# A hybrid decoder layer on one core: another order around block B's groups, output rows turned back in pieces, decay and outer product in one operation

## The reference, cut to what matters

```python
def hybrid_layer(x, ...):
    h = rmsnorm(x, norm_mix_g)
    ...                                    # one projection of h feeds two mixers
    S_new, o_g = gla(...)                  # gated linear attention, per token: S = diag(a) S + k^T v,  o = q S
    o_d = diff_attn(...)                   # samples read a paged cache of 2048 keys and values each
    x = x + concat(o_g, o_d) @ w_out
    h2 = rmsnorm(x, norm_ffn_g)
    u = square(relu(h2 @ w_up))            # 1024 -> 4096
    return x + u @ w_down                  # 4096 -> 1024
```

## Time and profile before

| what | value |
|---|---|
| median of 3 runs | 1423.88 us (1423.36 to 1424.85) |
| the profiled execution | 1431.62 us, its span 1429.9 us |
| PE busy | 1364.5 us (95%), 8589 matmuls |
| DVE, ACT, POOL busy | 923.8, 579.3, 402.4 us |
| mean granted TensorE clock | 0.988 of full speed |
| chain that ended last | PE 54%, DVE 8%, ACT 4%, DMA 3% |
| DMA | mean 168 GB/s |

### The profile page before, as it was taken

One profiled execution on the slowest core, in us unless ns is written; L12 is line 12 of the kernel. 1 busy time (PEld: TensorE's weight loads), 2 busy tenths in 40 slices (PEclk: granted clock), 3 DMA queues, 4 the chain that ended last, 5 costly groups with the idle time before them and its releaser, 6 DMA issues.

```text
span 1429.9 us, 23899 instructions
## 1 busy us (share of the span) xinstructions
PE 1364.5 (95%) x8589; PEld 1130.2 (79%) x8589; DVE 923.8 (65%) x1625; ACT 579.3 (41%) x1081; POOL 402.4 (28%) x395
## 2 busy tenths in 40 slices
PE   7999999999999999998999999999998999999998
PEld 6767777776777767776766767667998999999998
DVE  5459757745657877648667565434456665777885
ACT  6444333314545553624234241323433554334532
POOL 2546614335533444352000000000332112320330
PEclk9999999999999999999999999999999999999999
DMA  7537735344345574567386575873553563233021
GB/s 267 152 119 233 227 115 165 122 149 133 98 140 169 198 261 127 185 224 235 120 269 229 178 255 182 274 242 120 182 196 118 207 211 114 89 119 115 34 90 60
DMA packets 125527, 240.33 MB, mean 168 GB/s; under 512 B 13593, under 2 KB 46650, under 8 KB 125410
## 3 DMA queue, kind: packets, MB, share of 16 engines
q1 hardware_dynamic: 116210, 214.69, 45.4%
q10 hardware_dynamic: 9200, 24.13, 5.1%
HBM read 197.64 MB, written 41.14 MB: 167 GB/s over the span
## 4 chain that ended last, share of the span: by engine, by line
PE 54%; DVE 8%; issue 4%; ACT 4%; DMA 3%; SPq 1%; POOL 1%; ACTq 0%; DVEq 0%; POOLq 0%
PE ps L85 16%; PE ps L87 15%; PE ps L86 15%; PE ps L3258 2%; PE ps L1495 2%; DMA vr<-in_cache_v 1%; PE ps L1532 1%; DVE uw_l L2020 1%; PE ps L1314 1%; DMA kr<-in_cache_k 1%; ACT uw_h L2014 1%; DVE part_l L2784 1%; DVE xt L2793 1%; PE ps L1516 1%; DMA raw_dn<-in_w_down 1%
## 5 line engine op out<-in xcount | busy, mean ns | idle before, releaser
L3023 POOL TENSOR_TENSOR kr<-kr,qb 128x512 f32<-128x512 f32 x128 | 172.8, 1363 | 174.2 <-DMA kr<-in_cache_k 174.2
L85 PE MATMUL ps<-x2hB,uw_h 128*128 128x264 f32 (+1 forms) x512 | 145.5, 284 | 1.7 <-issue 1.1
L86 PE MATMUL ps<-x2lB,uw_h 128*128 128x264 f32 (+1 forms) x512 | 144.6, 282 | 0.0
L87 PE MATMUL ps<-x2hB,uw_l 128*128 128x264 f32 (+1 forms) x512 | 144.4, 282 | 0.0
L85 PE MATMUL ps<-part_h,fh 128*128 128x264 f32 (+1 forms) x448 | 129.2, 288 | 12.0 <-DVE xt L2793 11.4
L87 PE MATMUL ps<-part_h,fl 128*128 128x264 f32 (+1 forms) x448 | 127.9, 286 | 0.0
L86 PE MATMUL ps<-part_l,fh 128*128 128x264 f32 (+1 forms) x448 | 127.9, 285 | 0.0
L85 PE MATMUL ps<-uh,dh 128*128 128x512 f32 x256 | 105.1, 411 | 7.1 <-DVE dl L2113 4.7
L3012 DVE TENSOR_REDUCE sd<-kr 128x8 f32<-128x512 f32 x128 | 85.0, 675 | 38.4 <-POOL kr L3023 38.3
L85 PE MATMUL ps<-x2hA,uw_h 128*128 128x512 f32 x256 | 106.5, 416 | 0.0
L2793 DVE TENSOR_TENSOR xt<-xt,ps 128x264 f32<-128x264 f32 (+1 forms) x224 | 86.6, 422 | 30.8 <-PE ps L87 30.0
(11 more groups left out here) (384 smaller groups left out, 3466.2 us busy)
## 6 DMA issues: line engine op xcount, KB each, us to landing
kr<-in_cache_k SPq DMA_DIRECT2D x128, 256.0 KB, 3.3
raw_up<-in_w_up_units SPq DMA_DIRECT2D x64, 512.0 KB, 4.9
vr<-in_cache_v SPq DMA_DIRECT2D x128, 256.0 KB, 3.4
raw_dn<-in_w_down SPq DMA_DIRECT2D x32, 512.0 KB, 6.6
raw_dn<-in_w_down ACTq DMA_DIRECT2D x32, 512.0 KB, 4.8
raw<-in_w_in_units SPq DMA_DIRECT2D x23, 512.0 KB, 5.0
raw_up<-in_w_out_units SPq DMA_DIRECT2D x16, 512.0 KB, 4.1
kept_up_low<-uw_l SPq DMA_DIRECT2D x16, 512.0 KB, 6.6
```

What stands on the lines that cost most here:

```text
L85: pe.matmul(out, lh, rh, start=first and n == 0, stop=False, skip_group_check=onto)
L86: pe.matmul(out, lh, rl, start=False, stop=False, skip_group_check=onto)
L87: ins = pe.matmul(out, ll, rh, start=False, stop=last and n == len(ks) - 1, skip_group_check=onto)
L3023: pool.tensor_tensor(k[:, :], k[:, :], qb[v // PAGES][:, :], ALU.mult).then_inc(k_multiplied, 1)
```

## The change

Six edits, all in the order or the form of work:

- Block A stores the low parts of tiles KT+2 to KT+15 only. The stores of KT and KT+1, which nothing reads, are left out, and the waits for stores are counted two later.
- The samples' recurrence has no decay on ACT. DVE does both in one `scalar_tensor_tensor` for each sample and pair of heads (128 x 128, the decay as a per-partition scalar), four in a round as before, and doesn't wait for ACT.
- In group 0, ACT makes the high parts of all four sums before the third tile's; DVE makes the low parts of S1, S3, S2 before the norm and S4 within it.
- In all later groups ACT's split of tile t+3 stands before a square and DVE's `own(3)` before `change(T1, 1)`; `own(5)` moves from after n = 5 to after n = 9, the next A12 from after n = 23 to after n = 27, the last addition.
- The last group's products go P1, P2, P6, P7, P4, P5, P3.
- The rows are turned back in eight pieces, most of them between the last products, and stored in eight.

```diff
@@ feed_first, sync @@
-            if t == KT:
+            if t == KT + 2:
                 for i in range(2):
                     sp.wait_ge(up_out[i], STORED)
...
-            if t == KT - 1:
-                keep_low(KT)
...
-                if t + 1 < KT + FT * KEPT_GROUPS:
+                if KT + 2 <= t + 1 < KT + FT * KEPT_GROUPS:
                     keep_low(t + 1)
@@ products @@
     if g == FGROUPS - 1:
-        return [(x, j) for x in ("P1", "P6", "P2", "P7", "P5", "P4", "P3") for j in range(PAIRS)]
+        return [(x, j) for x in ("P1", "P2", "P6", "P7", "P4", "P5", "P3") for j in range(PAIRS)]
@@ feed_last @@
+    LAST = FGROUPS - 1
+    pieces = [(0, 0, KT), (1, 0, KT), (2, PAIRS, KT), (3, PAIRS, KT), (4, PAIRS, KT), (2, 0, PAIRS), (4, 0, PAIRS), (3, 0, PAIRS)]
+    BY_DVE = (3, 0, PAIRS)
@@ feed_last, tensor @@
+        def beside_last(x, j):
+            if x == "P5" and j in (1, 2):
+                pe.wait_ge(added, added_no(LAST, "P4", PAIRS - 1))
+                turn(pieces[j - 1], range(KT))
+            elif (x, j) == ("P3", 1):
+                pe.wait_ge(added, added_no(LAST, "P5", PAIRS - 1))
+                for i in (2, 3, 4):
+                    pe.wait_ge(*copied(pieces[0 if i < 4 else 1]))
+                    turn(pieces[i], range(PAIRS, KT))
+            elif (x, j) == ("P3", 2):
+                pe.wait_ge(added, added_no(LAST, "P3", 1))
+                pe.wait_ge(*copied(pieces[1]))
+                for i in (5, 6, 7):
+                    turn(pieces[i], range(2))
+            elif (x, j) == ("P3", 3):
+                for k in (2, 3):
+                    pe.wait_ge(added, added_no(LAST, "P3", k))
+                    for i in (5, 6, 7):
+                        turn(pieces[i], [k])
...
-                if g == FGROUPS - 1 and (x, j) == ("P3", 2):
-                    turn_y(0)
-        for t in range(1, 5):
-            turn_y(t)
+                if g == LAST:
+                    beside_last(x, j)
@@ feed_last, scalar @@
             high_factor(g, "A22")
             if g == 0:
+                for name in SUMS:
+                    high_factor(g, name)
                 split_high(act, t + 2)
...
-                split_high(act, t + 3)
-            high_factor(g, "S1")
-            high_factor(g, "S3")
+            else:
+                high_factor(g, "S1")
+                high_factor(g, "S3")
...
             square(g, 1, 0)
             high_part(g, "U11", 1)
-            square(g, 1, 1)
             if g:
                 split_high(act, t + 3)
+            square(g, 1, 1)
             high_part(g, "T1", 1)
@@ feed_last, vector @@
         def norm():
...
+            low_factor(0, "S4")
             dve.wait_ge(norm_rooted, 2)
...
             if g == 0:
+                for name in SUMS[:3]:
+                    low_factor(g, name)
                 norm()
...
+            own(3)
             change(g, "T1", 1)
-            own(3)
...
-                if n == 5:
+                if n == 9:
                     own(5)
...
-                if n == 23 and KEPT_GROUPS <= g + 1 < FGROUPS:
+                if n == 27 and KEPT_GROUPS <= g + 1 < FGROUPS:
                     low_factor(g + 1, "A12")
@@ sample_recurrence, scalar @@
-        for x in range(NS):
-            for t in range(2):
-                act.activation(st_new[:, x, t, :], st_new[:, x, t, :], ACT.Copy,
-                               scale=decay_s[:, 2 * x + t:2 * x + t + 1]).then_inc(st_updated, 1)
@@ sample_recurrence, vector @@
-        dve.wait_ge(st_updated, 2 * NS)
...
-            for t in range(2):
-                for hf in range(2):
-                    r, h = rows[hf], 2 * t + hf
-                    v = st_new[r, 2 * r_:2 * r_ + 2, t, :]
-                    ins = dve.tensor_tensor(v, v, ps[r, 5:7, h * DV:(h + 1) * DV], ALU.add)
+            for x in (2 * r_, 2 * r_ + 1):
+                for t in range(2):
+                    v = st_new[:, x, t, :]
+                    ins = dve.scalar_tensor_tensor(v, v, decay_s[:, 2 * x + t:2 * x + t + 1], ps[:, 5 + x % 2, t * DV:(t + 1) * DV],
+                                                   ALU.mult, ALU.add)
```

More of the change, by code:

```diff
@@ L2397, in out_tile, with turned, copied, piece_banks @@
         return o, tokens(0 if x in ("P1", "P2", "P4") else 1)
[L2399 to L2403, removed]
+    LAST = FGROUPS - 1
+    pieces = [(0, 0, KT), (1, 0, KT), (2, PAIRS, KT), (3, PAIRS, KT), (4, PAIRS, KT), (2, 0, PAIRS), (4, 0, PAIRS), (3, 0, PAIRS)]
+    BY_DVE = (3, 0, PAIRS)
+    def turned(piece):
+        return y_turned, 4 + pieces.index(piece) + 1
+    def copied(piece):
+        if piece == BY_DVE:
+            return added, DOWN0 + 7 * PAIRS * FGROUPS + 1
+        return y_copied, 4 + pieces.index(piece) + 1
+    def piece_banks(piece):
+        t, k0, k1 = piece
+        if t < 2:
+            return 2 * t
+        return (0, 1, 2)[t - 2] if k0 else (3, 4, 5)[t - 2]
+    def piece_rows(piece):
+        t, k0, k1 = piece
+        return ys[:, k0 * P:k1 * P] if t == 4 else yB[:, t, k0 * P:k1 * P]
+    def piece_in(piece):
+        t, k0, k1 = piece
+        b, n = piece_banks(piece), NS if t == 4 else P
+        if k1 - k0 == KT:
+            return ps[0:n, b:b + 2, :].rearrange("p b n -> p (b n)")
+        return ps[0:n, b, :]
     ALL = slice(0, N)
@@ L2449, in load_down, with store_y @@
             sp.dma_start(raw(x), a["w_down"][f:f + P, :]).then_inc(dn_in[x], 16)
[L2451 to L2454, removed]
+        def store_y(i):
+            t, k0, k1 = piece = pieces[i]
+            sp.wait_ge(*copied(piece))
+            rows = a["y_sample"] if t == 4 else a["y_prompt"][HALF + t * P:HALF + (t + 1) * P, :]
+            sp.dma_start(rows[:, k0 * P:k1 * P], piece_rows(piece)).then_inc(sem(f"y_out{i % 2}"), 16)
         for t in range(KT):
@@ L2552, in product, with turn @@
             ins.then_inc(down_ready, 1)
[L2554 to L2567, removed]
+        def turn(piece, ks):
+            t, k0, k1 = piece
+            n, b = NS if t == 4 else P, piece_banks(piece)
+            for k in ks:
+                c = (k - k0) * P
+                ins = pe.transpose(ps[0:n, b + c // 512, c % 512:c % 512 + P], xt[:, k, t * P:t * P + n], m["ident"][:, :])
+            if k == k1 - 1:
+                ins.then_inc(y_turned, 1)
+        def beside_last(x, j):
[17 more added lines that the diff above has]
+                        turn(pieces[i], [k])
         for v in range(KT):
@@ L2619, in high_part, with copy_y @@
             act.activation(part_place(name, k, False), part_source(name, k), ACT.Copy).then_inc(u_high, 1)
[L2621 to L2625, removed]
+        def copy_y(piece):
+            act.wait_ge(*turned(piece))
+            act.activation(piece_rows(piece), piece_in(piece), ACT.Copy).then_inc(y_copied, 1)
         for v in range(KT):
@@ L2689, in scalar @@
                 high_factor(g + 1, "A12")
-        for t in (0, 2, 4):
-            copy_y(t)
+        for piece in pieces:
+            if piece != BY_DVE:
+                copy_y(piece)
     def gpsimd(pool):
@@ L2875, in vector @@
                     low_factor(g + 1, "A11")
[L2876 removed]
+                if n == 27 and KEPT_GROUPS <= g + 1 < FGROUPS:
                     low_factor(g + 1, "A12")
[L2878 to L2879 removed]
+        dve.wait_ge(*turned(BY_DVE))
+        dve.tensor_copy(piece_rows(BY_DVE), piece_in(BY_DVE)).then_inc(added, 1)
     return {"sync": sync, "tensor": tensor, "scalar": scalar, "gpsimd": gpsimd, "vector": vector}
@@ L3573, in _ @@
                 run("sync", sp)
-                for t in range(5):
-                    m["store_yB"](t)
+                for i in range(8):
+                    m["store_yB"](i)
                 f["stored"](sp)
                 sp.wait_ge(sem("state_stored"), 48)
-                sp.wait_ge(sem("y_out0"), 80)
-                sp.wait_ge(sem("y_out1"), 64)
+                sp.wait_ge(sem("y_out0"), 96)
+                sp.wait_ge(sem("y_out1"), 96)
             @block.tensor
```

46 lines of the change are left out of this document (22 added, 24 removed).

## The result

The changed kernel takes 1408.3 us (median of 4 runs, 1407.0 to 1409.4), the kernel before 1423.85 us beside it: ratio 0.9887, 95% interval 0.9873 to 0.9902, so 15.6 us faster. The forecast was 1405.6 us with a range of 1399.5 to 1411.5 us: right in sign and inside the range, 2.7 us too low.

A forecast was written before the change was run, and what follows sets the result against it. PE was busy 95% of the span, so only its idle and low-clock time could be won. Terms 2.5 + 6.0 + 9.1 + 0 + 0.7 = 18.3 us, from 1423.88 to 1405.6 us; range 1399.5 to 1411.5 us.

The forecast's parts named there:

- Stores left out: Block A's norm: key load lands sooner, PE waits less before the spread and regains clock; 2.5 us, bounds 0 to 3.8.
- the clock's share comes back too: Around block A's norm: PE's clock of 0.79 over 8 us returns to full, worth 1.7 us.
- the prediction's own signs: Prediction called wrong if groups 3 to 6 reach 20.5 us, DVE waits for keys after 650 us, or PE waits absorb large gains.
- Decay and outer product: Samples' recurrence: one fused DVE operation removes DVE's 4.10 us and PE's 4.13 us waits; 6.0 us, bounds 4.0 to 6.8.
- a sign that the prediction had named against itself: Samples' recurrence: DVE waiting for keys after 650 us would show the prediction wrong.
- Group 0: Block B's group 0: low parts made during idle time bring products to group 1's time; 9.1 us, bounds 7.0 to 9.3.
- Groups 3 to 6: Block B's groups 3 to 6: moved `own(5)` gains nothing, other shifts cancel; 0 us, bounds -4 to +5.
- the late A11: Groups 3 to 6: DVE waits 3.31 us for A11, hanging on a late `raw_dn` load, taking back `own(5)`'s 1.2 us.
- The end: Last group and tail: no 1.13 us wait, later last product, shorter tail; +0.7 us, bounds -0.5 to +1.8.
- The groups in full: Rival for groups 3 to 6: next A11 doesn't bind, five microseconds more gained, 1400.6 us; chance 0.13.
- the key loads: Rival in the samples' recurrence: DVE waits for keys instead of ACT, only 2 us left, 1409.6 us; chance 0.10.
- slower than before: Rival in groups 3 to 6: A12, A22 and S1 each wait a whole POOL sum, 1434.4 us; chance 0.02.

The follow-up runs named there:

- early loads: Changed kernel with SP issuing the four `raw_dn` loads of groups 4 to 7 ahead of the up-tile load that waits for `own(4)`: 1411.7 us, ratio 0.9909.

## Why the prediction was right

The parts measured alone add up: 7.1 + 8.6 - 2.1 + 2.0 - 0.4 = 15.2 us, the whole change 15.6 us. Step by step:

- *Stores left out*, 2.5 us forecast (0 to 3.8): -0.4 us alone (-1.7 to 0.7), 1.3 to 2.7 us by the traces. The mechanism was right up to the spread: PE's wait fell from 2.10 us to 0.88 us (0.6 to 1.1 forecast), the key load to 4.5 us. The term that failed is "the clock's share comes back too", 1.7 us. The slow clock cost nothing in the kernel before, since what PE lost to it was PE's next wait, for ACT's attention weights (9.74 us from spread to L1532 at either clock). I had read the clock beside the norm and not asked what PE waits for next. The share was also taken over all 8 us of the window, in which PE was busy for 6.41 us. By the prediction's own signs this place counts as one where another wait of PE absorbs a part of the gain. Why the part is smaller in the times than in the traces stays open.
- *Decay and outer product*, 6.0 us forecast (4.0 to 6.8): 7.1 us (5.1 to 9.1), 4.6 to 5.2 us by the traces. A round took 1.11 us (1.0 forecast), and there was no idle time before the second round. PE's next wait was 2.25 us in the changed kernel and 0.73 us in the one with this part alone, where 1.2 us were forecast: in the first, two of DVE's low parts took 2.08 and 1.88 us beside POOL's key products. DVE did wait for a key product after 650 us in three of the seven kernels with this part (0.58 to 1.42 us, not in the changed one), a sign that the prediction had named against itself; no time was lost by it that a trace shows.
- *Group 0*, 9.1 us forecast (7.0 to 9.3): 8.6 us (6.7 to 10.3), 20.30 us for the products as said. Here the clock's share was real: behind those products nothing else waited.
- *Groups 3 to 6*, 0 forecast (-4 to +5): -2.1 us (-3.7 to -0.7). That the late A11 takes back what `own(5)` gives was right: the move alone gave nothing (ratio 0.9998), and with early loads it pays 4.5 us by the traces. Mis-sized was the cost of the later A12, "about 0.4 us later" and cancelled by `own(3)`: moved alone it cost 2.0 us (0.4 to 3.6), 1.5 us by the traces, since A22 and S1 come later and with them the up tiles of each next group. With all edits the loss of 1.6 us lies mostly in the products (88.8 against 87.5 us), which this doesn't explain. In the changed kernel PE's wait at P2 with j = 2 was 1.41 us in group 5 but only 0.3 us in group 6, where I had placed one of 1 us.
- *The end*, 0.7 us forecast (-0.5 to 1.8): 2.0 us (0.6 to 3.6). The last product came 1.4 us later against the group's start, near the 1.7 us forecast; behind it only 4.9 us followed, not 6.7 to 7.0 us. I had kept 3.7 us from the last issue to the end; with the last stores in pieces it took 2.55 us.
- *Rivals.* The groups in full, the key loads, and slower than before all fell. A12's place did cost, by DVE's own order and S1's meeting with the fourth sum.

The sum came out 2.7 us too large: three terms too high by 2.9, 0.5 and 2.1 us, two too low by 1.1 and 1.3 us, which makes 3.1 us, within what the measurements of five parts allow. That the total came so near is in part luck: misses of 5.5 us on one side and 2.4 us on the other cancel in it.

## What to carry to other kernels

In block A's norm a slow clock cost little, and in group 0 it cost all that it seemed to. So look at PE's next wait behind the slow stretch, and at which of the slow matmuls another engine waits for, before its share is counted. When an operation is moved away from in front of a wait and nothing comes of it, follow the next wait back to its load, and that load back to what its queue stands behind; here one reordering on SP together with one wait on POOL was worth half as much as the whole change. And a load that comes early wakes every engine that waited for it: the early loads alone lost some 3 us, since POOL's sums then met DVE in the critical stretch.

## What the runs showed of the hardware

Where DVE and POOL meet, the one that comes second seems to wait for the first: `own(4)` began 0.4 us behind a sum of POOL's and took 3.08 us in place of 1.22 us, a sum behind a DVE low part 3.23 to 3.31 us in place of 2.40 us, and POOL's power took 2.01 us when DVE's low part had begun 0.09 us before it, 1.02 us when it was POOL that began 0.12 us ahead (the kernel with early loads). Additions that read PSUM kept 0.36 us apiece. The Trainium skill, "GPSIMD Engine Reference", section 1 (Specifications), says that GpSimd shares its SBUF interfaces with VectorE; the trace agrees, and the price is in these rows alone.

In the last group 34 transposes stand among the products, 18 of them between 1399.1 and 1402.0 us, and the granted clock stayed at 1.00. The Trainium skill, "TensorE: Matmul & The Clock Gate", Part 4, says that transposes don't count as busy in the same way for the clock; nothing of that is to be seen in this amount. And the clock behind block A's norm sum differed between executions of the same work. In the eight kernels with the old stores it was, from 9 to 13 us behind the sum, 1.00 in four and 0.72, 0.77, 0.78 and 0.79 in the other four, while PE's way from the spread to L1532 was 9.74 or 9.75 us in five of them and at most 10.58 us.
